# Loading residual rows a tile earlier per stage, moving three tiles' statistics to ScalarE and adding the last tile's residual rows on TensorE

## What is computed

```python
gates = ...            # router: top-1 group, top-2 of its 4 experts, 16 experts in all
h = silu(x @ w_gate[e]) * (x @ w_up[e]) * gates[:, e]     # D_EXPERT = 512
ffn = sum_e h @ w_down[e]
out = layer_norm(ALPHA * x + ffn, ln2_g, ln2_b)           # ALPHA = 2 ** 0.25
```

## Time and profile before

| | |
|---|---|
| median of three runs | 978.63 us |
| the profiled execution, its own time | 974.39 us |
| its span | 972.6 us |
| busy: TensorE, VectorE, ScalarE, GpSimd | 92%, 70%, 58%, 36% of the span |
| chain that ended last | TensorE 57%, VectorE 18%, DMA 11%, issue 6%, ScalarE 6% |
| granted clock of TensorE, mean | 0.975 of full speed |

### The profile page before, as it was taken

The page is one execution under the profiler, slowest core; times in us unless marked ns, Lnnn a source line. Parts: engine busy times, 40 slices in busy tenths (PEclk is TensorE's granted clock), DMA queues, the critical chain, the costliest instruction groups (busy, mean ns, idle before and its releaser), DMA issues.

```text
span 972.6 us, 16090 instructions
## 1 busy us (share of the span) xinstructions
...
## 2 busy tenths in 40 slices
...
DMA packets 64959, 173.63 MB, mean 179 GB/s; under 512 B 19809, under 2 KB 35169, under 8 KB 52592
## 3 DMA queue, kind: packets, MB, share of 16 engines
...
## 4 chain that ended last, share of the span: by engine, by line
PE 57%; DVE 18%; DMA 11%; issue 6%; ACT 6%; SPq 1%; DVEq 0%; ACTq 0%; POOLq 0%; POOL 0%
PE ps L484 14%; PE ps L486 14%; PE ps L485 14%; DMA raw<-in_w_gate 10%; DVE junk_dve L1586 6%; PE ps L880 3%; PE ps L850 3%; DVE wlo L1898 2%; DVE bias L1534 2%; PE ps L867 1%; PE ps L1025 1%; ACT whi L1354 1%; ACT junk_act L1191 1%; DVE sm L1739 1%; ACT probs L1262 1%
## 5 line engine op out<-in xcount | busy, mean ns | idle before, releaser
L1898 DVE TENSOR_TENSOR wlo<-raw,whi 128x2048 fp32r<-128x2048 f32 x94 | 211.8, 2288 | 52.5 <-ACT whi L1354 52.3
L1354 ACT CAST whi<-raw 128x2048 fp32r<-128x2048 f32 x96 | 180.4, 1911 | 48.3 <-DMA raw<-in_w_gate 18.8
L484 PE MATMUL ps<-whi,xgT_hi 128*128 128x512 f32 x384 | 153.1, 399 | 7.5 <-DVE xgT_lo L1908 5.5
L486 PE MATMUL ps<-whi,xgT_lo 128*128 128x512 f32 x384 | 151.0, 393 | 0.0
L485 PE MATMUL ps<-wlo,xgT_hi 128*128 128x512 f32 x384 | 150.9, 393 | 0.0
L484 PEld LDWEIGHTS ps<-whi,xgT_hi 128*128 128x128 f32 x384 | 73.1, 190 | 23.6 <-issue 9.1
L484 PE MATMUL ps<-xT_hi,w_hi 128*128 128x512 f32 (+1 forms) x232 | 88.7, 382 | 1.1 <-DVE w_lo L1471 1.1
L2120 POOL COPY idx_now<-slot_token 128x1 int32 (+1 forms) x24 | 8.8, 366 | 222.0 <-PE ps L1025 211.7
L485 PE MATMUL ps<-xT_lo,w_hi 128*128 128x512 f32 (+1 forms) x232 | 87.6, 378 | 0.0
L486 PE MATMUL ps<-xT_hi,w_lo 128*128 128x512 f32 (+1 forms) x232 | 87.6, 378 | 0.0
L486 PEld LDWEIGHTS ps<-whi,xgT_lo 128*128 128x128 f32 x384 | 72.9, 190 | 15.7
...
## 6 DMA issues: line engine op xcount, KB each, us to landing
...
```

The costliest lines, as they stand in the source:

```text
L484: pe.matmul(out, l_hi, r_hi, start=start, stop=False)
L486: return pe.matmul(out, l_lo, r_hi, start=False, stop=stop)
L1354: act.copy(whi[:, n, :], raw[:, n, :]).then_inc(gu_hi if n < 4 else dn_hi, 1)
L1898: dve.tensor_tensor(wlo[:, n, :], raw[:, n, :], f32(whi[:, n, :]), ALU.subtract).then_inc(gu_lo if n < 4 else dn_lo, 1)
```

## The change

Rows of the eight tiles are loaded by ScalarE's queue (`load_rows`) when the adds of tiles 0 to 20 have landed, in front of tile 22's `gated`; the two parameter rows ride in the same queue. Rows of tiles 6 and 7 and the third-last tile's rows go to `late_rows`, in the space of the first weight buffers. Tile 21's rows are added to `acc_d` after that load, and gathered as an eleventh tile (`THIRD`). Tile 22's products are no longer added in DRAM: VectorE adds them to the gathered rows `xg` (`prev_added`), and TensorE adds to tile 23's down products the rows of tile 22's tokens that are in both (`same_token`, a 128x128 matrix of ones and zeros, times `ysb`) and the gathered rows `xc` (times `ident`), four fp32 matmuls ahead of the 24 of `down`; the sum starts in PSUM (`begun`), and is normalised there. For tiles 4, 5 and 7 ScalarE takes mean and variance in two passes (`row_stats`) in place of VectorE. The steps of the ends are interleaved by hand with the last two tiles' work on VectorE and ScalarE. The register loops of ScalarE and VectorE end one tile earlier, GpSimd's too. Three indirect stores take the place of two. The tokens' comparison moves ahead, its matmuls (now two) to tile 0. Each expert gets at least one tile. Some semaphores of earlier stages are merged.

```diff
@@ -199,6 +199,8 @@
 EARLY = 2
+THIRD, PREV, LAST = NT, NT + 1, NT + 2
+BY_SCALAR = (4, 5, 7)
 RING = {"pt", "rl", "pw", "cm", "cv", "cb"}
@@ -310,15 +312,19 @@
+token_f = at("token_f", [P, 3], F32, 77.875)
+in_both, in_later = (at(n, [P, 1], F32, kb) for n, kb in (("in_both", 77.9375), ("in_later", 77.625)))
+same_token = at("same_token", [P, P], F32, END + 1.25)
+late_rows = at("late_rows", [P, 3, D], F32, SC)
+junk_rows = at("junk_rows", [P, D], F32, SC + 12)
+idx_out = [at(f"idx_out{i}", [P, 1], I32, 77.6875 + 0.0625 * i) for i in range(3)]
+idx_row = [at(f"idx_row{i}", [P, 1], I32, 77.375 + 0.0625 * i) for i in range(2)]
+ln2_g = at("ln2_g", [P, D], F32, R2)
+ln2_b = at("ln2_b", [P, D], F32, R2 + 4)
@@ -494,9 +500,15 @@
   return xa[:, t, :] if t < 4 else xb[:, t - 4, :]
-def last_rows(n):
-  return x1_tile(n) if n < NT else (xg, xc)[n - NT][:]
+def norm_rows(n):
+  if n < 6:
+    return xa[:, n, :] if n < 4 else xb[:, n - 2, :]
+  return late_rows[:, n - 6, :] if n <= THIRD else (xg, xc)[n - PREV][:]
+def stats_by_dve(n):
+  return n - sum(q < n for q in BY_SCALAR)
 N_UNITS = len(UNITS)
@@ -678,22 +690,11 @@
   if_fresh(TILES - 1, down)
...
   for t in range(NT):
     sp.wait_ge(fin_done, t + 1)
-    sp.dma_start(a["out"][0, t * P:(t + 1) * P, :], x1_tile(t)).then_inc(out_done, 16)
+    sp.dma_start(a["out"][0, t * P:(t + 1) * P, :], norm_rows(t)).then_inc(out_done, 16)
   sp.wait_ge(out_done, 16 * NT)
-  sp.wait_ge(rows_out, 32)
+  sp.wait_ge(rows_out, 48)
 @block.tensor
@@ -1054,7 +1055,7 @@
                                  whi[:, 4 + n, col:col + 512], wlo[:, 4 + n, col:col + 512],
-                                 ft == 0, ft == FT - 1)
+                                 ft == 0 and not begun, ft == FT - 1)
       last.then_inc(dn_used, 1)
@@ -1080,6 +1081,11 @@
   hidT(0)
+  pe.wait_ge(both_in, 1)
+  for i in range(2):
+    last = pe.matmul(ps[:, 7, i * P:(i + 1) * P], token_f[:, i:i + 1].to_broadcast([P, P]), ident[:],
+                         start=True, stop=True)
+  last.then_inc(both_mm, 1)
   pe.wait_ge(experts_set, 1)
@@ -1094,10 +1100,17 @@
   pe.wait_ge(both_in, 2)
-  pe.wait_ge(hid_set, last_t + 1)
-  pe.matmul(ps[:, 0, 0:P], token_f[:, 0:1].to_broadcast([P, P]), ident[:], start=True, stop=True
-       ).then_inc(both_mm, 1)
-  down(last_t, loads(last_t))
+  for c in range(2):
+    part = slice(c * 512, (c + 1) * 512)
+    pe.wait_ge(prev_added, c + 1)
+    if c:
+      pe.wait_ge(y_set, last_t)
+    pe.matmul(pair(1)[:, part], same_token[:], ysb[:, part], start=True, stop=False)
+  pe.wait_ge(rows_in[2], 16)
+  for c in range(2):
+    part = slice(c * 512, (c + 1) * 512)
+    pe.matmul(pair(1)[:, part], ident[:], xc[:, part], start=False, stop=False)
+  down(last_t, loads(last_t), begun=True)
 @block.scalar
@@ -1302,12 +1315,30 @@
   def norm_sd(n):
-    act.wait_ge(stat, 3 * n + 3)
-    act.activation(rstd2[:, n % 2:n % 2 + 1], mv2[:, n % 2, 1:2], ACT.Sqrt, bias=eps2).then_inc(ln_sd, 1)
+    if n in BY_SCALAR:
+      act.wait_ge(stat_act, 2 * BY_SCALAR.index(n) + 2)
+      act.activation(rstd2[:, n:n + 1], mv2[:, n, 1:2], ACT.Sqrt, bias=eps2, scale=1.0 / D).then_inc(ln_sd, 1)
+    else:
+      act.wait_ge(stat, 3 * stats_by_dve(n) + 3)
+      act.activation(rstd2[:, n:n + 1], mv2[:, n, 1:2], ACT.Sqrt, bias=eps2).then_inc(ln_sd, 1)
+  def row_stats(n):
+    i = BY_SCALAR.index(n)
+    act.wait_ge(rows_at[n], 32)
+    if i:
+      act.wait_ge(stat_act, 2 * i)
+    else:
+      act.wait_ge(rows_at[7], 32)
+    act.activation(junk_rows[:], norm_rows(n), ACT.Identity, scale=1.0 / D, accum_out=mv2[:, n, 0:1]
+                       ).then_inc(stat_act, 1)
+    act.wait_ge(stat_act, 2 * i + 1)
+    act.activation(junk_rows[:], norm_rows(n), ACT.Square, scale=-1.0, bias=mv2[:, n, 0:1],
+                       accum_out=mv2[:, n, 1:2]).then_inc(stat_act, 1)
   def norm_scale(n):
     act.wait_ge(ln_rstd, n + 1)
-    act.activation(last_rows(n), last_rows(n), ACT.Copy, scale=rstd2[:, n % 2:n % 2 + 1]).then_inc(ln_scaled, 1)
+    act.activation(norm_rows(n), norm_rows(n), ACT.Copy, scale=rstd2[:, n:n + 1]).then_inc(ln_scaled, 1)
   def parts_copy(t):
@@ -1404,41 +1435,78 @@
   gated(1)
-  def tile(t):
+  def tile(t, before, early, after):
     x_hi_part(t)
     split_new(t, [3])
-    y_part(t - 2)
-    h_hi_part(t - 1)
-    split_new(t - 1, (4, 5), t - 2)
-    split_new(t + 1, range(3))
-    gated(t)
+    y_part(early)
+    h_hi_part(before)
+    split_new(before, (4, 5), early)
+    split_new(after, range(3))
+  def load_rows():
+    last_load = act.value_load(expert_of[0:1, bass.ds(last_t, 1)], min_val=0, max_val=EXPERTS - 1)
+    act.wait_ge(x1_out, 16 * NT)
+    act.wait_ge(acc_out, 16 * NT)
+    act.wait_ge(y_out, third_t * 16)
+    for t in range(NT):
+      if t == 6:
+        act.wait_ge(gu_lo, last_load * 4 + 2)
+      act.dma_start(norm_rows(t), acc_d[(t + 1) * P:(t + 2) * P, :]).then_inc(rows_at[t], 16)
+      if t in (1, 3):
+        act.dma_start((ln2_g if t == 1 else ln2_b)[:], a["ln2_g" if t == 1 else "ln2_b"][0].partition_broadcast(P)
+               ).then_inc(ln2_in, 16)
   prev_t = act.value_load(prev_tile, min_val=MIN_TILES - 2, max_val=TILES - 2)
   third_t = act.value_load(third_last, min_val=MIN_TILES - 3, max_val=TILES - 3)
-  tile(2)
+  fourth_t = act.value_load(fourth_last, min_val=MIN_TILES - 4, max_val=TILES - 4)
+  tile(2, 1, 0, 3)
+  gated(2)
   with act.Fori(3, TILES) as t:
-    with act.If(t <= prev_t):
-      tile(t)
+    with act.If(t <= third_t):
+      tile(t, t - 1, t - 2, t + 1)
+      gated(t)
+  tile(prev_t, third_t, fourth_t, prev_t + 1)
+  load_rows()
+  gated(prev_t)
   x_hi_part(last_t)
   split_new(last_t, [3], prev_t)
+  norm_sd(0)
   y_part(third_t)
   h_hi_part(prev_t)
+  norm_sd(1)
   split_new(prev_t, (4, 5), third_t)
+  norm_scale(0)
+  norm_scale(1)
+  row_stats(4)
+  norm_sd(2)
+  row_stats(5)
   gated(last_t)
...
   act.copy(pair(2), ln2_g[:]).then_inc(gain_set, 1)
-  norm_sd(0)
-  norm_scale(0)
-  norm_sd(1)
-  y_part(prev_t)
+  norm_sd(3)
+  norm_sd(4)
+  norm_sd(5)
+  norm_scale(2)
+  act.wait_ge(dn_used, prev_t * 2 + 2)
+  act.wait_ge(y_out, prev_t * 16)
+  act.copy(ysb[:, 0:512], ps[:, 2, :]).then_inc(gain_set, 1)
+  act.copy(ysb[:, 512:], ps[:, 3, :]).then_inc(y_set, 1)
   h_hi_part(last_t)
   split_new(last_t, (4, 5), prev_t)
-  norm_scale(1)
-  for n in range(2, NT + 1):
-    norm_sd(n)
-    norm_scale(n)
-  norm_sd(NT + 1)
+  norm_scale(3)
+  norm_sd(6)
+  norm_scale(4)
+  row_stats(7)
+  norm_sd(7)
+  norm_scale(5)
+  norm_scale(6)
+  norm_sd(THIRD)
+  norm_scale(7)
+  norm_sd(PREV)
+  norm_scale(THIRD)
+  norm_sd(LAST)
 @block.vector
@@ -1724,34 +1792,53 @@
-  def norm_gain(n, x):
-    mv, rstd = mv2[:, n % 2, :], rstd2[:, n % 2:n % 2 + 1]
-    if n >= 2:
-      dve.wait_ge(ln_scaled, n - 1)
+                                     ).then_inc(fix_set, 1)
+  def norm_stats(n):
+    if n < NT:
+      dve.wait_ge(rows_at[n], 32)
+    elif n == THIRD:
+      dve.wait_ge(rows_in[0], 16)
+    elif n == LAST:
+      dve.wait_ge(dn_used, last_t * 2 + 2)
+    done = 3 * stats_by_dve(n)
+    if n:
+      dve.wait_ge(stat, done)
+    x = pair(1) if n == LAST else norm_rows(n)
     for c in range(2):
       dve.bn_stats(stats[:, c, :], x[:, c * 512:(c + 1) * 512]).then_inc(stat, 1)
-    dve.wait_ge(stat, 3 * n + 2)
-    dve.bn_aggr(mv, stats).then_inc(stat, 1)
-    dve.wait_ge(stat, 3 * n + 3)
+    dve.wait_ge(stat, done + 2)
+    dve.bn_aggr(mv2[:, n, :], stats).then_inc(stat, 1)
+  def norm_gain(n):
+    x = pair(1) if n == LAST else norm_rows(n)
+    if n in BY_SCALAR:
+      dve.wait_ge(stat_act, 2 * BY_SCALAR.index(n) + 2)
+    else:
+      dve.wait_ge(stat, 3 * stats_by_dve(n) + 3)
     if n == 0:
+      dve.wait_ge(ln2_in, 32)
+    if n == 4:
       dve.wait_ge(gain_set, 1)
-    dve.scalar_tensor_tensor(x, x, mv[:, 0:1], pair(2), ALU.subtract, ALU.mult)
+    dve.scalar_tensor_tensor(x, x, mv2[:, n, 0:1], ln2_g[:] if n < 4 or n == LAST else pair(2), ALU.subtract, ALU.mult)
+  def norm_inverse(n):
     dve.wait_ge(ln_sd, n + 1)
-    dve.reciprocal(rstd, rstd).then_inc(ln_rstd, 1)
+    dve.reciprocal(rstd2[:, n:n + 1], rstd2[:, n:n + 1]).then_inc(ln_rstd, 1)
@@ -1821,7 +1908,7 @@
   link(dve.tensor_reduce(ntile[:, 1:], over, AX.X, ALU.add))
-  link(dve.tensor_scalar(ntile[:, 1:2], ntile[:, 1:2], 1.0, None, ALU.max))
+  link(dve.tensor_scalar(ntile[:, 1:], ntile[:, 1:], 1.0, None, ALU.max))
   link(dve.tensor_tensor_scan(cum, ones17, ntile, 0.0, ALU.mult, ALU.add))
@@ -1929,14 +2017,18 @@
   last_t = dve.value_load(last_tile, min_val=MIN_TILES - 1, max_val=TILES - 1)
+  prev_t = dve.value_load(prev_tile, min_val=MIN_TILES - 2, max_val=TILES - 2)
+  third_t = dve.value_load(third_last, min_val=MIN_TILES - 3, max_val=TILES - 3)
+  link(dve.tensor_scalar(spare_row[:], slot_token[:], float(P), 1.0e6, ALU.is_lt, ALU.mult))
+  link(dve.scalar_tensor_tensor(out_row[:], spare_row[:], -float(P), slot_token[:], ALU.add, ALU.add))
+  for i, t in enumerate((last_t, prev_t)):
```

(113 more changed lines are left out.)

103 lines of the change are left out of this document (14 added, 89 removed).

## The result

The median of 11 runs is 982.06 us (978.18 to 983.90), beside 977.76 for the kernel before (11 runs, 971.39 to 980.17): a ratio of **1.0043, 95% interval 1.0023 to 1.0062**. The forecast was 973.6 with a range from 969.5 to 980.5. The profiled execution took 978.18, its span is 976.5 us (before 972.6). Most of the difference lies at the end: from silu(21), the last that the old loop and the new one share, to the end of the span it is 81.49 us (976.5 - 895.01) against 78.97 (972.6 - 893.63). I call this stretch the **tail** (silu(n) and hid(n) are ScalarE's and VectorE's operations of that name in tile n); as the work in front of it differs from one profile to the next (silu(21) starts between 891.82 and 900.70 in those of this study), profiles are compared by it. The other 1.4 us are there before the tail begins; what they come from stays open.

What follows compares the result with a forecast made beforehand. VectorE was taken to bound the last 75 us; after the change GpSimd would set the end. Span 967.3 plus 0.3 contention gave 967.6, -5.0 against 972.6; taken to the median, 973.6, range 969.5 to 980.5.

Steps and rivals of the forecast that it cites:

- chain of row dependencies: Tail: tile 20's add lands 908.9, rows in 924.1, tile 21's add lands 931.6, gathers and first bias add done 937.8.
- cover of VectorE: End of kernel: VectorE done at 958.0, covered by 3 us because GpSimd's last indirect store starts at 961.3.
- The landing and the row loads: Before tile 22's `gated`: tile 20's add lands at 908.9, ten issues end at 913.4, rows in at 924.1; low ends taken.
- its 1.6 of waits: GpSimd's bias adds after 937.8: 1.6 us added because ScalarE's scales 3 and 5 are late.
- the `xg` addition: VectorE, tile 22: products added at 941.0, so TensorE's fp32 matmuls start then and tile 23's down products end at 950.5.
- Contention: VectorE's `xg` product beside GpSimd's bias adds: up to 0.9 us each on a few operations; 0.3 added.
- Sum: End of kernel: last indirect store 961.3, 6.0 behind it, span 967.3; with 0.3 added 967.6, -5.0 against 972.6.
- Early edits at nothing: Before tile 0's `hidden` on VectorE: moved work of 1.5 us fits 2.84 of idle time, costing nothing on the path.
- Rival 1: ScalarE, 918 to 941, falls behind, with table loads costing twice 1.28: 3.8 later, time 977.4; chance 0.17.
- Rival 2: TensorE's clock falls to 1.2 GHz after its gap from 938 to 941: time 979.4, or 974.9 if half hit; chance 0.07.
- Rival 3: ScalarE's queue held by `load_rows` before `gated(22)`, delaying silu and all behind: +3.5, 982.1; chance 0.13.
- Moving statistics to ScalarE: VectorE in the tail loses the statistics of three tiles, 4.5 us; ScalarE takes 2.7 per `row_stats`.

Runs made afterwards that it cites:

- run 6: Changed kernel with the loads of ln2_g and ln2_b issued ahead of the wait for tile 20's add: ratio 1.0012 to the kernel before, tail 80.0 us.
- run 7: Changed kernel with the statistics of rows 4, 5 and 7 computed by VectorE again: ratio 1.0036 to the kernel before, tail 80.22 us.
- run 3: Changed kernel with GpSimd's gathers for the last two tiles ahead of the third last's gather and first bias add: ratio 1.0044, tail 82.19 us.
- run 1: Changed kernel with the last-but-one tile's final `xg` product reading ln2_b from a PSUM copy: ratio 1.0015 to the kernel before, tail 79.55 us.
- runs 4, 5: 4: changed kernel, early register loads and token copies moved back, ratio 1.0023. 5: kernel before with that early edit alone, ratio 1.0008.

## Why the prediction was wrong

The direction was wrong because the sum followed VectorE's and GpSimd's amount of work and took the chain of row dependencies (add, row loads, add, gathers) at its best values, step by step. Two steps failed. One is that chain: its late links put the end of GpSimd's list 6.5 us behind the forecast, 5.1 of them within the tail. The other is the cover of VectorE, whose last product for `xg` was to lose 0.9 at most and lost 4.3.

- *The landing and the row loads*, the term that was mis-sized most. Tile 20's add started at 904.58 (forecast 902.7) and its landing was seen at 912.1 (908.9): 7.5 us, not the 6.2 taken from the earlier trace rows. GpSimd's issue took 3.15 instead of 1.61, beside VectorE's split of weights; from its end to the landing it was 4.4, no more than the 4.6 of before. Rows were in at 929.47 (924.1), 17.3 after the landing where 15.2 was forecast; the ten issues took 5.4 instead of 4.4, and what made the rest isn't shown. Of the 5.4 us, 1.4 were there before the tail, 0.5 more at the add's start, 1.3 are its landing and 2.1 the loads. The prediction took the low ends "since the DMA engines have nothing else to do"; but not only traffic makes these steps slow.
- *GpSimd.* The gathers began at 939.08, forecast 931.6: 5.4 from the rows, 1.3 from the second slow add (7.5 again), 0.8 between its landing and the gather's start. From there the list went as forecast, even without its 1.6 of waits, and ended at 964.49 (958.0).
- *VectorE, the `xg` addition*: forecast at about 941 behind ScalarE's copy, it came at 948.99 behind a gather issued at 943.62 that takes 5.3 to land. TensorE's down products thus ended at 961.9, forecast 950.5.
- *Contention*: "up to 0.9 each on a few operations; VectorE's share is covered" was wrong in size and place. It was 4.3 us on one product with no cover. The forecast drew its bound from two examples and didn't ask how long GpSimd's run of adds is. The Trainium skill ("SBUF — State Buffer", SBUF: two separate sides) says that the pair shared by the two engines goes to the one that starts first for its whole instruction; that agrees with the held copy of run 6 and with run 7, where the turn came at the end of the add that was running, while run 3, against the 1.28 of run 1, shows more: four GpSimd instructions in a row kept VectorE out.
- *Sum.* The last store started at 970.53 instead of 961.3: 6.5 from GpSimd's late list (1.4 of them from before the tail), 2.7 from VectorE, which was to have 3 us of cover and came last.
- *Early edits at nothing*: cover 2.84, cost put at 1.5. The register loads alone lie in 2.18 us of idle time ahead of L2022, and hid(0) came 1.0 late; how much of it the end sees is open (runs 4, 5).
- *ScalarE.* Table loads cost 1.28, and at two of the three switches the next operation is 0.01 behind, one of them back to silu in mid-work; at the first (919.21) it waited for VectorE. So the trace does not agree with the 1.38 of drain that the Trainium skill ("ScalarE: Activation LUTs", What ACT_TABLE_LOAD costs) adds. Rival 1 falls as a mechanism, not in its size: silu(23) was 4.2 late (939.82 against 935.6; 1.4 of these from before the tail), since the square roots in front of it waited for VectorE, and that for ln2_b; with the norm loads first (run 6) it comes 42.3 after silu(21) instead of 44.8. The end did not see it: VectorE's `xg` addition waited longer for the gather.
- *Rival 2* happened (clock at 0.50 from 945), under cover. *Rival 3* had the right sign and its trigger (silu(22) at 917.69, behind 916) but the wrong place: the delay ran through GpSimd and the DMA engines, not through silu. That its 982.1 is so near to the measured 982.06 is luck: it took 10.1 for the landing and 0.915 for an issue, measured were 7.5 and about 0.5. *Moving statistics to ScalarE* was priced as a gain of 4.5 and is worth nothing (run 7), since VectorE had idle time right there.
